# The value stage of a mixture-of-experts kernel: weights split by four keys instead of two, and four places for streamed table tiles instead of five

## The chip, the cores and the metric

The kernel runs on one core of a Trainium2 chip. It is timed as device microseconds of one launch. Three timed runs of the kernel before gave a median of 2621.04 us (2620.36 to 2621.34).

## What is computed

One decoder block on 256 tokens of width 2048: gated linear attention and sparse attention side by side, cross-attention to a memory, and a feed-forward layer of single-neuron experts (PEER). The change touches the last step of that layer. Each token chose 16 experts in each of 8 heads out of 128 x 128; its output is the weighted sum of the experts' rows of the table `peer_v` (16384 x 2048):

```python
def block(args):
    xb, eb, gb = args
    act = jax.nn.gelu(jnp.einsum('td,tkd->tk', xb, u_tab[eb]))
    return jnp.einsum('tk,tkd->td', gb * act, v_tab[eb])
```

The last step of the program adds this to the residual and applies an RMSNorm.

## The kernel before

**The value stage.** Most of the output is made without a gather. The table `peer_v` is read as a whole, as 128 tiles of 128 rows by 2048 columns (1024 KB), one for each first-half key j. For each key there is a matrix of weights, 128 rows of the tile by tokens, in `spread` (128 columns) and `spread_shared` (64 more), and TensorE adds up weights times tile into all eight PSUM banks. To keep float32 precision, tile and weights are each split into a high and a low part of the fast matmul type:

- ScalarE writes the tile's high part in two halves (`value_high`, L1355; `v_hi` has two places), VectorE the low part over it (`value_low`, L2425; `v_lo` lies where `v_raw` lay).
- ScalarE writes the high part of the weights (`weights_high`, L1366, copies of L1374), VectorE the low part (`weights_low`, L2431, L2434), into `e_parts`, two batches of BATCH keys each.
- TensorE runs `high_pass(i)` (L1813, 12 matmuls of L1824), then `low_pass(i - 1)` (L1828, 8 matmuls of L1836). The end of a low pass signals `tile_used`: the tile's place is free.

**Who fetches.** SyncE issues the tiles in the order of the keys (L812 to L825). Tile j waits for the low pass of the tile that had its place before (`tiles_freed`), five keys back. The first five wait each for what lay in their place: dots of the stage before, two steps of the octet copies ("unit_spread"), and, for key 4, "seeded", when the residual has been read into the banks.

**The late rows.** For the last four heads of the second 128 tokens, rows are gathered singly: GpSimd issues 64 indirect DMAs for rows of `peer_u` and 64 for rows of `peer_v` (`late_rows`, L884), 128 partitions of 8 KB each, and VectorE works on one of them for nearly every key (`late_step`: a dot product, L2446, or a multiply-add into `hN`, L2453; both a little over 2 us). Rows have three places at first; a fourth opens at row 37 and a fifth at row 71, which lie in `spread_shared` where the weights of the first 32 and 64 keys were. So these two wait for "e_split", which counts batches of weights that are split (`ROWS_GROW`).

**Order on each engine.** It is written out by hand. VectorE at key j: weights of the next batch, if j is the last of its batch; the low part of tile j; the late row. ScalarE at key j: the high part of tile j; then the weights of the next batch, if j is the last of its batch, which waits for the low pass of the batch that had the place before (`tiles_freed` in `weights_high`). A high half of tile i waits for the high pass and for the low part of tile i - 2, whose place in `v_hi` it takes.

```python
V_PLACES = (RAW + 104 * K, HT + 8 * K, HT, MRG + 8 * K, WRK)
```

These are the tiles' five places in SBUF. `e_parts` begins at MRG.

Of the kernel before, what the change touches and what calls it, by code (L numbers as in the profile page):

```python
# [50 lines left out]
GROUPS = TT * PEER_H  # L51
RING = 6
RING_IN_QUERIES = 4
BATCH = 2
VCOLS = D // 2
BANK = 512
LATE = tuple(range(GROUPS - 4, GROUPS))
# [3 lines left out]
SPLIT = tuple(j for j in range(NKEYS) if j not in NATIVE)  # L61
LATE_FROM = 1
LATE_SPAN = NKEYS - 2
ROWS_GROW = {37: 16, 71: 32}
UNIT = 4
SHARED = P // 2
HALF = P // UNIT
# [132 lines left out]
def hybrid_block(nc, a):  # L200
# [4 lines left out]
    def sem(name):  # L205
        if name not in sems:
            sems[name] = ctx.enter_context(nc.semaphore(name))
        return sems[name]

    base = (nc.sbuf_base + 63) // 64 * 64  # L210
    K = 1024

    def sb(name, shape, at, dt=F32):

        return nc.alloc_sbuf_tensor_at("b_" + name, [P] + list(shape), dt, offset=base + int(at))[:]


    RAW, HI, LO, ACTV, ATTN, HT, SCR, MRG, WRK, SML = (0, 32 * K, 48 * K, 64 * K, 96 * K, 128 * K, 144 * K, 160 * K,
                                                       176 * K, 192 * K)
# [86 lines left out]
        + [(SCR, n) for n in range(4)])]  # L306
    e_whole = sb("e_whole", [2, BATCH, 3 * P], MRG)
    e_parts = sb("e_parts", [2, BATCH, 3 * P], MRG, F32R)
    E_HI, E_LO, E_SHARED = slice(0, P), slice(P, 2 * P), slice(2 * P, 3 * P)
    E_SHARED_HI, E_SHARED_LO = slice(2 * P, 2 * P + SHARED), slice(2 * P + SHARED, 3 * P)  # L310
    V_PLACES = (RAW + 104 * K, HT + 8 * K, HT, MRG + 8 * K, WRK)
    v_raw = [sb(f"v_raw{n}", [D], at) for n, at in enumerate(V_PLACES)]
    v_lo = [sb(f"v_lo{n}", [D], at, F32R) for n, at in enumerate(V_PLACES)]
    v_hi = sb("v_hi", [2, D], SCR, F32R)
# [69 lines left out]
    def load_chunk(sp, apart, p, c, w, col):  # L384
        rows = w.rearrange("(q k p) n -> q p k n", q=UQ, p=P)
        for q in range(UQ):
            apart(w_split, unit(p, c, q) - 2 * UQ + 1)
            sp.dma_start(raw[:, UQ * c + q], rows[q][:, :, bass.ds(col, CH)]).then_inc(w_landed[UQ * c + q], 16)

    def load_pair(sp, apart, p, sources):  # L390
        for c, (w, col) in enumerate(sources):
            load_chunk(sp, apart, p, c, w, col)
# [7 lines left out]
    def load_wide(sp, apart, p, w, col):  # L400
        rows = w.rearrange("(u k p) n -> u p k n", u=2 * UQ, p=P)
        for u in range(2 * UQ):
            apart(w_split, unit(p, 0, u) - 2 * UQ + 1)
            sp.dma_start(as_wide(raw[:, u]), rows[u][:, :, bass.ds(col, WIDE)]).then_inc(w_landed[u], 16)
# [268 lines left out]
    def slot_free(s):  # L673

        return max(dotted_at(n) for n in range(EARLY * PTOP) if row_slot[n] == s)
# [12 lines left out]
    def places(count, first, grow):  # L688

        place, back = [], []  # L690
        size = first
        for n in range(count):
            size += n in grow
            place.append(n if n < first else size - 1 if n in grow else place[n - size])
            back.append(size)
        return place, back

    tile_place, tile_back = places(NKEYS, len(v_raw), {})
    row_place, row_back = places(LATE_ROWS, 3, ROWS_GROW)

    def landed(sems, place, n):
        return sems[place[n]], 16 * place[:n + 1].count(place[n])
# [8 lines left out]
    def tiles_freed(eng, *tiles):  # L711

        eng.wait_ge(sem("tile_used"), 1 + max(use_order.index(j) for j in tiles))
# [9 lines left out]
    def weights_of(b):  # L723

        split = [j for j in range(b * BATCH, (b + 1) * BATCH) if j not in NATIVE]
        keys = slice(split[0], split[-1] + 1)
        e = e_parts[:, b % 2, split[0] % BATCH:split[-1] % BATCH + 1]
        def by_unit(x):
            return x.rearrange("p i (u t) -> p i u t", t=UNIT)
# [30 lines left out]
    def square(name):  # L760
        return a[name][0]
# [4 lines left out]
    @block.sync  # L766
    def _(sp):
        apart = Apart(sp, w_split)
        for half in range(2):
            d = slice(half * D // 2, (half + 1) * D // 2)  # L770
            sp.dma_start(xN[:, :, d], a["x"][0, :, d].rearrange("(t p) d -> p t d", p=P)).then_inc(sem(f"x_landed{half}"), 16)

        def load_small(dst, name, w, done):
            sp.dma_start(small_w[:, :, dst:dst + w],
                         w_in[:, COL[name]:COL[name] + w].rearrange("(k p) n -> p k n", p=P)).then_inc(done, 16)

        load_small(0, "i_k", IDX_D, sem("keys_in"))
        load_small(P, "d_k", DH, sem("keys_in"))
        load_chunk(sp, apart, IQ, 0, w_in, COL["i_q"])
        load_small(2 * P, "d_v", DH, sem("small_landed"))  # L780
        load_small(3 * P, "i_w", IDX_H, sem("small_landed"))
        load_small(3 * P + IDX_H, "g_low", RANK, sem("small_landed"))
        load_chunk(sp, apart, IQ, 1, w_in, COL["i_q"] + CH)
        load_pair(sp, apart, IQ + 1, [(w_in, COL["i_q"] + (2 + c) * CH) for c in range(2)])

        def stream(first, lo, hi, w, col=0):
            with sp.Fori(lo, hi) as i:
                load_pair(sp, apart, first + i, [(w, i * 2 * CH + col + c * CH) for c in range(2)])

        def gated(first, gate, w):  # L790
            with sp.Fori(0, 4) as i:
                load_wide(sp, apart, i * 2 + first, w_in, i * WIDE + COL[gate])
                load_wide(sp, apart, i * 2 + first + 1, w, i * WIDE)

        stream(DQ, 0, 4, w_in, COL["d_q"])
        gated(GB, "gate_b", square("w_proj_dsa"))
        with sp.Fori(0, GLA_H) as h:
            load_pair(sp, apart, h * 3 + GL, [(w_in, h * DK + COL[n]) for n in ("g_q", "g_k")])
            load_wide(sp, apart, h * 3 + GL + 1, w_in, h * DV + COL["g_v"])
            load_pair(sp, apart, h * 3 + GL + 2, [(w_in, h * DV + COL["g_r"] + c * CH) for c in range(2)])  # L800
        gated(GA, "gate_a", square("w_proj_gla"))
        for first, name in ((XK, "w_xk"), (WO, "w_out")):
            stream(first, 0, 4, square(name))
        with sp.Fori(0, 4) as i:
            load_wide(sp, apart, XV + i, square("w_xv"), i * WIDE)
        for first, name in ((XQ, "w_xq"), (XO, "w_xo"), (PQ, "peer_wq")):
            stream(first, 0, 4, square(name))

        v_rows = a["peer_v"][0]

        for j in range(NKEYS):
            if j == 0:  # L812
                sp.wait_ge(sem("dotted"), slot_free(5))
            if j == 1:
                sp.wait_ge(sem("dotted"), EARLY * PTOP)
            if j == 2:
                sp.wait_ge(sem("unit_spread"), HALF + 4)
            if j == 3:
                sp.wait_ge(sem("unit_spread"), HALF + 8)
            if j == 4:  # L820
                sp.wait_ge(sem("seeded"), 2)
            if j >= tile_back[j]:
                tiles_freed(sp, j - tile_back[j])
            where, count = landed(v_landed, tile_place, j)
            sp.dma_start(v_raw[tile_place[j]], v_rows[j * P:(j + 1) * P]).then_inc(where, 16)  # L825
        sp.wait_ge(sem("late_used"), LATE_ROWS)
        sp.dma_start(gfin, a["norm_final_g"].partition_broadcast(P)).then_inc(sem("final_gain_landed"), 16)
        for t in range(TT):
            for n in range(4):
                sp.wait_ge(sem("out_ready"), 4 * t + n + 1)  # L830
                sp.dma_start(a["out"][0, t * P:(t + 1) * P, n * 512:(n + 1) * 512], hN[:, t, n * 512:(n + 1) * 512]
                             ).then_inc(sem("out_stored"), 16)
        sp.wait_ge(sem("out_stored"), 16 * TT * 4)
# [3 lines left out]
    def _(pool):  # L837
# [46 lines left out]
        def late_rows(lo, hi):  # L884

            pool.wait_ge(sem("dotted"), slot_free(4) if hi == 1 else EARLY * PTOP)
            for m in range(lo, hi):
                g, kind, k = LATE[m // (2 * PTOP)], m // PTOP % 2, m % PTOP
                if m in ROWS_GROW:
                    pool.wait_ge(sem("e_split"), ROWS_GROW[m])  # L890
                elif m >= 3:
# [19 lines left out]
    def _(act):  # L911
# [454 lines left out]
        def weights_high(b):  # L1366

            if b >= 2:
                tiles_freed(act, *range((b - 2) * BATCH, (b - 1) * BATCH))
            for j in range(b * BATCH, (b + 1) * BATCH):  # L1370
                if j in NATIVE:
# [1198 lines left out]
```

## Time and profile before

| | |
|---|---|
| median of three runs | 2621.04 us |
| the profiled execution | 2621.42 us, its span 2619.7 us |
| TensorE matmul busy | 2308.6 us (88%) |
| VectorE busy | 2026.9 us (77%) |
| ScalarE busy | 1304.5 us (50%) |
| GpSimd busy | 655.9 us (25%) |
| DMA moved | 729.10 MB, mean 278 GB/s |
| value stage | about 1966 to 2601 us of the span |

The profile is one execution. "Idle before" names the engine or DMA that ended an instruction's wait. A DMA's "us to landing" counts from its issue on the queue to its last byte's signal, so it holds the time in which it queues behind other transfers. In the timeline a row of SPq is the issue alone.

### The profile page before, as it was taken

The numbers are of one execution on the slowest core, as the hardware profiler recorded it, in microseconds if no ns is written. First come the engines' busy times: TensorE is split into PE (matmuls) and PEld (weight loads), VectorE is DVE, ScalarE is ACT, GpSimd is POOL, SyncE is SP. The second block draws the span as 40 slices with busy tenths as digits, with TensorE's granted clock in tenths as the row PEclk, the third lists the DMA queues.
The fourth block names the chain that finished last, engine by engine and source line by source line (L and its number), as shares of the span: only waits on it lengthen the run. The fifth ranks groups of instructions, "written<-read, shape, count | busy, mean of one in ns | idle before, by whom it ended". The sixth has DMA issues, their size and how long they took to land.

```text
span 2619.7 us, 35803 instructions
## 1 busy us (share of the span) xinstructions
PE 2308.6 (88%) x13097; PEld 2021.1 (77%) x13097; DVE 2026.9 (77%) x2622; ACT 1304.5 (50%) x2085; POOL 655.9 (25%) x339
## 2 busy tenths in 40 slices
PE   8999999999999999999999775536329999999997
PEld 7998889999988888889989765435227777777775
DVE  7786556667655755664467999999999999999999
ACT  4555544444444543454355324887645444444444
POOL 1000000000000000010001577886853343345331
PEclk9999999999999999999999987666659999999999
DMA  7444665554566555564457999999989999999997
GB/s 232 147 141 142 193 193 169 161 161 149 172 213 186 182 189 187 175 208 154 144 178 268 356 394 414 421 422 391 408 313 395 421 421 421 421 419 421 421 421 310
DMA packets 273975, 729.10 MB, mean 278 GB/s; under 512 B 21192, under 2 KB 164768, under 8 KB 215856
## 3 DMA queue, kind: packets, MB, share of 16 engines
q1 hardware_dynamic: 226432, 385.65, 42.8%
q0 software_dynamic: 46912, 340.81, 31.9%
q8 instruction: 85, 1.39, 0.2%
q10 hardware_dynamic: 496, 0.84, 0.1%
q14 instruction: 50, 0.41, 0.0%
HBM read 725.14 MB, written 2.10 MB: 278 GB/s over the span
## 4 chain that ended last, share of the span: by engine, by line
PE 57%; DMA 20%; DVE 16%; ACT 3%; POOL 3%; issue 2%; SPq 0%; DVEq 0%; ACTq 0%; POOLq 0%
PE bank L429 20%; PE bank L451 15%; PE bank L478 10%; DMA b_v_raw<-in_peer_v 7%; DVE b_u_ring L2368 7%; DMA b_late_row<-in_peer_v,b_idx_all 5%; DMA b_late_row<-in_peer_u,b_idx_all 4%; DMA b_u_ring<-in_peer_u,b_idx_all 3%; PE bank L1824 3%; POOL b_u_ring L880 2%; PE bank L1836 2%; DVE b_late_row L2446 1%; PE bank L1613 1%; DVE b_hN L2453 1%; DVE b_v_lo L2429 1%
## 5 line engine op out<-in xcount | busy, mean ns | idle before, releaser
L415 DVE TENSOR_TENSOR b_w_both<-b_raw,b_w_both 128x1024 fp32r<-128x1024 f32 x464 | 564.0, 1234 | 422.2 <-ACT b_w_both L410 421.1
L410 ACT ACTIVATE b_w_both<-b_raw 128x1024 fp32r<-128x1024 f32 x464 | 483.4, 1057 | 538.7 <-PE bank L429 215.1
L880 POOL DMA_INDIRECT b_u_ring<-in_peer_u,b_idx_all x192 | 381.9, 1989 | 159.5 <-DVE b_dots L2368 75.3
L1824 PE MATMUL bank<-b_v_hi,b_e_parts 128*128 128x512 f32 x1536 | 385.0, 397 | 33.0 <-DVE b_e_parts L2434 20.8
L1364 ACT ACTIVATE b_v_hi<-b_v_raw 128x1024 fp32r<-128x1024 f32 x254 | 255.2, 1052 | 307.8 <-DVE b_v_lo L2429 158.7
L2368 DVE CUSTOM_DVE_ANT_0 b_u_ring<-b_u_ring,b_xnN 128x2048 f32<-128x2048 f32 x172 | 390.7, 2278 | 12.9 <-DMA b_u_ring<-in_peer_u,b_idx_all 12.7
L1824 PEld LDWEIGHTS bank<-b_v_hi,b_e_parts 128*128 128x128 f32 x1536 | 283.4, 189 | 122.4 <-issue 33.0
L429 PE MATMUL bank<-b_w_both,b_act_both 128*128 128x512 f32 x1536 | 353.7, 390 | 0.0
L429 PEld LDWEIGHTS bank<-b_w_both,b_act_both 128*128 128x128 f32 x1536 | 287.3, 188 | 59.3
L451 PE MATMUL bank<-b_act_both,b_w_both 128*128 128x256 f32 x2688 | 329.1, 284 | 0.0
L451 PEld LDWEIGHTS bank<-b_act_both,b_w_both 128*128 128x128 f32 x2688 | 324.4, 192 | 1.6 <-issue 1.3
L2429 DVE TENSOR_TENSOR b_v_lo<-b_v_raw,b_v_hi 128x2048 fp32r<-128x2048 f32 x128 | 291.9, 2281 | 0.0
L1836 PE MATMUL bank<-b_v_lo,b_e_parts 128*128 128x512 f32 x1024 | 253.4, 390 | 0.0
L1836 PEld LDWEIGHTS bank<-b_v_lo,b_e_parts 128*128 128x128 f32 x1024 | 192.4, 188 | 40.7
L451 PE MATMUL bank<-b_att_both,b_w_both 128*128 128x256 f32 x1536 | 188.3, 284 | 0.0
L451 PEld LDWEIGHTS bank<-b_att_both,b_w_both 128*128 128x128 f32 x1536 | 185.5, 192 | 0.2
L478 PE MATMUL bank<-b_act_both,b_w_both 128*128 128x512 f32 (+1 forms) x1024 | 181.6, 338 | 0.0
L429 PE MATMUL bank<-b_w_both,b_att_both 128*128 128x512 f32 x768 | 177.1, 392 | 0.0
L478 PEld LDWEIGHTS bank<-b_act_both,b_w_both 128*128 128x128 f32 x1024 | 158.2, 190 | 21.7
L894 POOL DMA_INDIRECT b_late_row<-in_peer_v,b_idx_all x64 | 125.3, 1957 | 191.9 <-DVE b_hN L2453 135.8
L894 POOL DMA_INDIRECT b_late_row<-in_peer_u,b_idx_all x64 | 120.5, 1883 | 206.5 <-DVE b_dots L2446 140.3
L429 PEld LDWEIGHTS bank<-b_w_both,b_att_both 128*128 128x128 f32 x768 | 145.2, 189 | 30.7 <-issue 0.3
(326 smaller groups left out, 2504.3 us busy)
## 6 DMA issues: line engine op xcount, KB each, us to landing
b_v_raw<-in_peer_v SPq DMA_DIRECT2D x128, 1024.0 KB, 11.1
b_raw<-in_w_in SPq DMA_DIRECT2D x208, 512.0 KB, 4.6
b_raw<-in_w_proj_dsa SPq DMA_DIRECT2D x32, 512.0 KB, 4.9
b_raw<-in_w_proj_gla SPq DMA_DIRECT2D x32, 512.0 KB, 4.0
b_raw<-in_w_xk SPq DMA_DIRECT2D x32, 512.0 KB, 3.4
b_raw<-in_w_out SPq DMA_DIRECT2D x32, 512.0 KB, 3.4
b_raw<-in_w_xv SPq DMA_DIRECT2D x32, 512.0 KB, 4.4
b_raw<-in_w_xq SPq DMA_DIRECT2D x32, 512.0 KB, 4.2
```

The costliest lines, as they stand in the source:

```text
L410: act.activation(w_hi[:, q], raw[:, UQ * c + q], ACT.Copy).then_inc(w_high, 1)
L415: dve.tensor_tensor(w_lo[:, q], raw[:, UQ * c + q], w_hi[:, q].bitcast(F32), ALU.subtract).then_inc(w_split, 1)
L429: mm = pe.matmul(bank[pair[t]], x[:, kt, t * P:(t + 1) * P], as_wide(w_both[:, half, u % UQ])[:, k], start=(kt == 0 and half == 0 and x is ...
L451: mm = pe.matmul(proj[c][:, n], w[:, q, k, n * P:(n + 1) * P], x[:, kt, :], start=(q == 0 and n == 0 and k == 0 and w is w_hi and x is hi) ...
L478: mm = pe.matmul(twin[c][n] if wide else twin[c][n][:, 0], *pair, start=wide and first, stop=not wide and last, skip_group_check=True)
L880: pool.indirect_dma_start(u_ring[:, s], None, u_rows, bass.IndirectOffsetOnAxis(ap=idx_all[:, at:at + 1], axis=0)).then_inc(u_landed[s], 16)
L894: pool.indirect_dma_start(late_row[row_place[m]], None, (u_rows, a["peer_v"][0])[kind], bass.IndirectOffsetOnAxis(ap=idx_all[:, g * PTOP + ...
L1364: act.activation(v_hi[:, v_place(i), c], v_raw[tile_place[j]][:, c], ACT.Copy).then_inc(sem("v_high"), 1)
L1824: mm = pe.matmul(value_bank(e is E_SHARED, v, m), e_parts[:, j // BATCH % 2, j % BATCH, e], v_hi[:, v_place(i), c:c + BANK], start=False, ...
L1836: mm = pe.matmul(value_bank(e is E_SHARED, v, m), e_parts[:, j // BATCH % 2, j % BATCH, e], v_lo[tile_place[j]][:, c:c + BANK], start=Fals ...
L2368: dve.tensor_tensor_reduce(u, u, xnN[:, g // PEER_H], 1.0, 0.0, ALU.mult, ALU.add, dots[:, g * PTOP + k:g * PTOP + k + 1]).then_inc(sem("d ...
L2429: dve.tensor_tensor(v_lo[tile], v_raw[tile], v_hi[:, v_place(i)].bitcast(F32), ALU.subtract).then_inc(sem("v_split"), 1)
```

## The change

Batches of weights hold four keys instead of two. `e_parts` becomes 12 KB instead of 6 and reaches into the place at MRG + 8 K, so this place for tiles goes away and four are left. The wait that stood ahead of the fourth tile ("unit_spread", 8 octets) goes with it, and "seeded" stands ahead of key 3 instead of key 4. The counts at which rows 37 and 71 get their places are converted to batches of four. No arithmetic changes, and no transfer is added or removed.

```diff
-BATCH = 2
+BATCH = 4
...
-ROWS_GROW = {37: 16, 71: 32}
+ROWS_GROW = {37: 32 // BATCH, 71: 64 // BATCH}
...
-    V_PLACES = (RAW + 104 * K, HT + 8 * K, HT, MRG + 8 * K, WRK)
+    V_PLACES = (RAW + 104 * K, HT + 8 * K, HT, WRK)
...
             if j == 2:
                 sp.wait_ge(sem("unit_spread"), HALF + 4)
             if j == 3:
-                sp.wait_ge(sem("unit_spread"), HALF + 8)
-            if j == 4:
                 sp.wait_ge(sem("seeded"), 2)
             if j >= tile_back[j]:
                 tiles_freed(sp, j - tile_back[j])
```

SyncE's queue at the start of the value stage, keys 0 to 6, before (`b_v_raw_147` to `_151` are the tiles' five places; the semaphore waited for stands in brackets):

```order
L825 DMA b_v_raw_147<-in_peer_v 128x2048 [waits dotted]
L825 DMA b_v_raw_148<-in_peer_v 128x2048 [waits dotted]
L825 DMA b_v_raw_149<-in_peer_v 128x2048 [waits unit_spread]
L825 DMA b_v_raw_150<-in_peer_v 128x2048 [waits unit_spread]
L825 DMA b_v_raw_151<-in_peer_v 128x2048 [waits seeded]
L825 DMA b_v_raw_147<-in_peer_v 128x2048 [waits tile_used]
L825 DMA b_v_raw_148<-in_peer_v 128x2048 [waits tile_used]
```

And of the change:

```order
L823 DMA b_v_raw_147<-in_peer_v 128x2048 [waits dotted]
L823 DMA b_v_raw_148<-in_peer_v 128x2048 [waits dotted]
L823 DMA b_v_raw_149<-in_peer_v 128x2048 [waits unit_spread]
L823 DMA b_v_raw_150<-in_peer_v 128x2048 [waits seeded]
L823 DMA b_v_raw_147<-in_peer_v 128x2048 [waits tile_used]
L823 DMA b_v_raw_148<-in_peer_v 128x2048 [waits tile_used]
L823 DMA b_v_raw_149<-in_peer_v 128x2048 [waits tile_used]
```

Key 3's tile now stands behind "seeded", and key 4's is the first that waits for a low pass, where key 5's was; each later issue waits for the same low pass as before with the next key's tile.

ScalarE from the first batch of weights on, before (`b_e_parts<-b_spread` and `<-b_spread_shared` are the weights' high parts, `b_v_hi` the tiles'):

```order
L1374 ACTIVATE b_e_parts<-b_spread 128x2x128 [waits spread_copied]
L1374 ACTIVATE b_e_parts<-b_spread_shared 128x2x64
L1364 ACTIVATE b_v_hi<-b_v_raw_148 128x1024 [waits v_landed1]
L1364 ACTIVATE b_v_hi<-b_v_raw_148 128x1024
L1374 ACTIVATE b_e_parts<-b_spread 128x2x128
L1374 ACTIVATE b_e_parts<-b_spread_shared 128x2x64
L1364 ACTIVATE b_v_hi<-b_v_raw_149 128x1024 [waits v_split,v_high_used,v_landed2]
L1364 ACTIVATE b_v_hi<-b_v_raw_149 128x1024
L1364 ACTIVATE b_v_hi<-b_v_raw_150 128x1024 [waits v_split,v_high_used,v_landed3]
L1364 ACTIVATE b_v_hi<-b_v_raw_150 128x1024
L1374 ACTIVATE b_e_parts<-b_spread 128x2x128 [waits tile_used]
L1374 ACTIVATE b_e_parts<-b_spread_shared 128x2x64
```

And of the change (lines are two lower):

```order
L1372 ACTIVATE b_e_parts<-b_spread 128x4x128 [waits spread_copied]
L1372 ACTIVATE b_e_parts<-b_spread_shared 128x4x64
L1362 ACTIVATE b_v_hi<-b_v_raw_148 128x1024 [waits v_landed1]
L1362 ACTIVATE b_v_hi<-b_v_raw_148 128x1024
L1362 ACTIVATE b_v_hi<-b_v_raw_149 128x1024 [waits v_split,v_high_used,v_landed2]
L1362 ACTIVATE b_v_hi<-b_v_raw_149 128x1024
L1362 ACTIVATE b_v_hi<-b_v_raw_150 128x1024 [waits v_split,v_high_used,v_landed3]
L1362 ACTIVATE b_v_hi<-b_v_raw_150 128x1024
L1372 ACTIVATE b_e_parts<-b_spread 128x4x128
L1372 ACTIVATE b_e_parts<-b_spread_shared 128x4x64
L1362 ACTIVATE b_v_hi<-b_v_raw_147 128x1024 [waits v_split,v_high_used,v_landed0]
L1362 ACTIVATE b_v_hi<-b_v_raw_147 128x1024
```

The second batch's pair has moved behind key 3's high part, pairs are twice as wide, and the pair that waited for "tile_used" ahead of key 4's high part is gone.

## Rows read from the trace of the kernel before

**Rows 1.** The page's GB/s moved, in 40 equal slices of the span.

```profile
GB/s 232 147 141 142 193 193 169 161 161 149 172 213 186 182 189 187 175 208 154 144 178 268 356 394 414 421 422 391 408 313 395 421 421 421 421 419 421 421 421 310
```

**Rows 2.** Stretches: us; busy PE, PEld, DVE, ACT, POOL (instructions); PEclk, DMA share, GB/s.

```profile
1948.00:1956.00 8.00, 8.00 (x50) 8.00 (x50) 7.32 (x29) 3.18 (x6) 0.00 (x0) 0.67 0.19 52
1956.00:1964.00 8.00, 8.00 (x70) 7.93 (x70) 8.00 (x30) 6.81 (x13) 1.47 (x2) 1.00 0.65 244
...
1972.00:1976.00 4.00, 4.00 (x19) 3.33 (x18) 4.00 (x3) 2.01 (x2) 1.80 (x1) 1.00 0.37 109
1976.00:1984.00 8.00, 8.00 (x37) 6.62 (x36) 8.00 (x9) 3.06 (x5) 3.79 (x3) 1.00 0.99 399
1984.00:2100.00 116.00, 110.08 (x474) 87.86 (x473) 109.69 (x83) 54.00 (x73) 43.54 (x23) 1.00 1.01 422
...
2400.00:2500.00 100.00, 96.52 (x404) 73.91 (x403) 95.51 (x73) 45.72 (x62) 36.58 (x20) 1.00 1.01 421
...
2593.00:2599.00 6.00, 5.84 (x25) 4.33 (x24) 6.00 (x4) 3.27 (x4) 0.00 (x0) 1.00 0.33 132
```

**Rows 3.** Timeline of SyncE's queue, 1957 to 1976 us: start, us, what.

```profile
1957.65 0.33 SPq L825 DMA_DIRECT2D b_v_raw<-in_peer_v  x1
...
1966.95 7.62 SPq L825 DMA_DIRECT2D b_v_raw<-in_peer_v  x2
```

**Rows 4.** Chain of waits, 2400 to 2425 us: start, us, what.

```profile
2399.04 13.86 DMA b_v_raw<-in_peer_v
...
2412.92 1.07 ACT b_v_hi L1364
...
2414.12 2.97 PE bank L1824 x12
2417.10 1.83 PE bank L1836 x8
...
2418.94 13.84 DMA b_v_raw<-in_peer_v
```

**Rows 5.** Value tiles landing, in 1930-2060, 1976-2000, 2100-2150, 2400-2500; a DMA issue.

```profile
DMA to landing us min/median/max: 6.8/10.0/11.2
...
DMA to landing us min/median/max: 8.4/8.4/8.4
...
DMA to landing us min/median/max: 10.0/10.1/10.3
...
DMA to landing us min/median/max: 13.8/13.8/13.9
...
b_gfin<-in_norm_final_g SPq DMA_DIRECT2D x1, 1024.0 KB, 4.7
```

**Rows 6.** Timeline, 2000 to 2040 us (as rows 3; idle before in brackets).

```profile
2003.89 2.01 ACT L1364 ACTIVATE b_v_hi<-b_v_raw 128x1024 fp32r<-128x1024 f32 x2 [4.44 <-DVE b_v_lo L2429]
...
2013.99 2.00 PE L1836 MATMUL bank<-b_v_lo,b_e_parts 128*128 128x512 f32 x8
...
2015.82 2.88 PE L1824 MATMUL bank<-b_v_hi,b_e_parts 128*128 128x512 f32 x12
```

**Rows 7.** Timeline at the stage's start, then VectorE from 1989 us.

```profile
1965.77 0.42 ACT L1374 ACTIVATE b_e_parts<-b_spread 128x256 fp32r<-128x256 f32 x1
1966.09 0.29 ACT L1374 ACTIVATE b_e_parts<-b_spread_shared 128x128 fp32r<-128x128 f32 x1
...
1966.29 1.99 ACT L1364 ACTIVATE b_v_hi<-b_v_raw 128x1024 fp32r<-128x1024 f32 x2
...
1989.90 0.42 DVE L2434 TENSOR_TENSOR b_e_parts<-b_spread,b_e_parts 128x256 fp32r<-128x256 f32 x1
...
1990.49 2.28 DVE L2429 TENSOR_TENSOR b_v_lo<-b_v_raw,b_v_hi 128x2048 fp32r<-128x2048 f32 x1
```

**Rows 8.** Who waited for whom, 1966 to 2600 us: total, times, longest.

```profile
PE bank L1824 <- DVE b_e_parts L2434: 20.8, 25, 5.5
```

**Rows 9.** Timeline of GpSimd, 2120 to 2180 us.

```profile
2139.59 2.42 POOL L894 DMA_INDIRECT b_late_row<-in_peer_u,b_idx_all  x1 [0.30 <-issue]
```

## The prediction

> **What bounds the kernel now.** I read the page's row of GB/s first: the DMA engines move more in the last third than anywhere else and stand at 421 GB/s for most of it [rows 1]. The table of stretches says from when: they move 52 GB/s from 1948 to 1956 us, 244 from 1956 to 1964, 109 from 1972 to 1976, then 399, and from 1984 on 421 to 422 with a share of 1.01, up to the last tiles at 2593 [rows 2]. So ahead of about 1976 us the engines have holes, and behind it none. The value stage takes, for each key, one tile of 1024 KB by SyncE's queue and, nearly always, one late row of the same size by GpSimd's: 2.10 MB at 421 GB/s are 4.98 us. The chain of waits shows the same pace from the other side: from the issue of one tile to the issue of the one four keys on are 19.90 us [rows 4], 4.975 us a key. In it a tile is under way for 13.86 us; the other 6.04 are ScalarE's first half (1.07), the high pass (2.97), the low pass of the key before (1.83) and gaps, and that low pass frees the place of the next issue. PE's part, 2.97 + 1.83 = 4.80 us, is shorter than 4.975, and VectorE is busy for 95.51 of 100 us there [rows 2]; both come close, neither is the bound.
>
> **The change part by part.** (a) *One place less at the start.* Before, the tile of key 3 has its place from the octet copies and is issued at 1957.65; key 4 and key 5 follow at 1966.95 and some 7.3 us later [rows 3]. The changed SyncE queue waits for "seeded" with key 3 (1966.95) and for the first low pass with key 4. All later issues stand where they stood, each with the next key's tile, so the stage has one tile less in hand. What was moved at 1957.65 was moved in a hole, and the engines have another hole at 1972 to 1976 after it [rows 2], so nothing queued behind makes up for it. One tile more must then be moved in the stretch without holes: 1.049 MB / 421 GB/s = 2.49 us. The bounds are 0, if the tile is caught up somewhere, and 4.98 us, if it costs a whole key. A gain is excluded, as no transfer is removed. I take 2.5, since what follows runs at 421 GB/s throughout.
>
> (b) *The first batch is twice as wide.* PE's first high pass waits for ScalarE's two copies. They start at 1965.77 and 1966.09, the next instruction at 1966.29 [rows 7]: 0.52 us the pair, 0.42 for 256 columns and 0.29 for 128. By that, 128 columns cost 0.13, and twice the width adds 0.26 + 0.13 = 0.39 us (bounds 0 and 0.52). PE starts that much later, and so do the first low pass and the issue that waits for it; the hole at 1972 grows. I take +0.4 us.
>
> (c) *Fewer and wider splits later.* Of 64 pairs each, 32 go away on ScalarE and 32 on VectorE. On VectorE a pair takes 0.59 us, from 1989.90 to 1990.49 [rows 7]; a merged pair costs between 0.59 and 1.18 in place of 1.18. Taking the middle, VectorE gains 0.3 us every four keys, some 9 us in all. ScalarE no longer waits for the tile of two keys back ahead of the split, but for that of four back, long done. PE waits 20.8 us in the stage for the weights' low parts [rows 8], and some of that goes. None of it reaches the end: the cover is the DMA at 4.975 us a key. I cost it at 0. If that cover were gone, it would be a gain of up to 9 us. In turn a merged split holds VectorE's and ScalarE's queues for up to twice as long once in four keys; queued behind it are the key's value split, its late row and the next key's high half. The low pass that needs the value split runs only after the next key's high pass, so that costs 0 too.
>
> (d) *One tile less in the loop.* This is the term on which the forecast stands. Before, the loop is 13.86 + 6.04 us for four keys; after, it closes over three, so the pace holds if a tile lands within 3 x 4.975 - 6.04 = 8.9 us. In the first half the chain is another: VectorE waits for late rows, ScalarE reads a tile at 2003.89 and its low pass is over at 2015.82, about 12 us [rows 6]; tiles land in 10.1 us and then wait [rows 5]. With four places 4 x 4.975 - 12 = 7.9 us are left. What is the landing time when one tile less is queued? The bounds are 4.7 us (the final gain, of the same size, on idle engines [rows 5]) and 13.86, as now. I take 8.9 and 7.9, no loss: the landing time beyond 4.7 is queueing at engines that are full, and it is the remainder of the loop, not its cause. It was 8.4 in the stage's first 24 us, with the same two queues but a shorter backlog, and 6.8 for the quickest tile [rows 5]. With one tile less, 4.975 us of waiting per tile go away, and about one to two tiles and two rows are still queued. The engines idle only if both queues run empty, and then a landing is short. Cost 0; the high end is a rival below.
>
> The Trainium skill, page "DMA: Bandwidth & Descriptors", section "Queues, rings and completion order", says that each DMA engine goes round-robin between the rings it has work for. By that rule SyncE's tile gets at least every second turn, and an estimate for a tile that finds its own ring empty is 2.5 us more than on idle engines, 7.2 us, under both limits. No row here shows the turns; the rule speaks for (d).
>
> (e) *Late rows 37 and 71.* They wait for the same keys' weights, now 8 batches of four in place of 16 of two, reached up to two keys earlier. GpSimd issued row 37 at 2139.59 after 0.30 us of its own issue, not of a wait [rows 9]: 0.
>
> **Sum.** 2.5 + 0.4 = +2.9 us. The profiled execution took 2621.42 us (span 2619.70), 0.38 above the median of the three timed runs; 2624.3 against it, 2623.9 against the median. A measurement of this kernel can tell about 0.2% (5.2 us) from no change, so this counts as no change.
>
> **The rivals.** *Slower: the tile stream runs out in the first half.* Mechanism: the 12 us hold of rows 6 stays, and a landing takes longer than 7.9 us because late rows keep the engines' turns. At 8.4 us a key takes (8.4 + 12)/4 = 5.10 us, 0.13 more, over 60 keys +8: 2632. At 10.1, as now, 5.5 us a key and +33 us: 2657. For it: the margin is thin (7.9 against 8.4 measured), and four keys' splits at once make the loop uneven. Against it: the engines would have to idle while tiles take as long as on full ones, and part of the 12 us is slack, as PE waits there for weights. It decides where the first half's DMA share drops below 1.0. Chance 0.20, most of it at the low end.
>
> *Faster: the instructions saved count.* If a full DMA share only reflects the pace that VectorE sets, the stage gains the 9 us of (c), less the 2.9: 2615. The Trainium skill, page "VectorE: DVE Perf Modes", section "The TRN2 errata — SBUF-src ops pay a fixed extra latency per instruction", says each such instruction carries a fixed cost, which merging saves; its (N+151)/0.96 ns fits the 0.42 us of 256 columns. An estimate by it is 0.31 us for each four keys. Against it: 422 GB/s is the most that any slice of the page shows [rows 1], and late in the stage ScalarE waits for tiles, not for VectorE, in the chain [rows 4]. Chance 0.04.
>
> *The lost tile is caught up.* PE's and VectorE's free 0.2 us a key can't bring bytes back, but the end can: if the last tile lands as early as now, 2621. It counts as no change, within the forecast's 0.76.
>
> **How the numbers follow.** Forecast 0.76 (within 0.2%), slower 0.20, faster 0.04. The range goes from 2620.5, a lost tile that costs nothing, to 2632, the slower rival at 8.4 us; that leaves out the faster rival and the slower one's upper part.
>
> **What would show it.** Right: the share stays 1.01 from 1984 on; the tiles' landing time falls to about 8 us in the first half and 9 in the second, and is no longer 13.8; three tiles to a loop of 14.9 us; issue of key 3's tile at about 1967; PE's first high pass 0.4 us later, the end 2 to 3 us later; VectorE's busy time down by some 9 us with no gain from it. Wrong: a DMA share under 1.00 in any stretch of the stage, ScalarE waiting more than 3 us for a tile, landing times still over 10 us, or a stage that ends earlier.

## The result, and the profile after

The changed kernel took 2653.86 us (four runs, 2650.71 to 2656.78), the kernel before 2620.70 (four runs, 2619.64 to 2621.34): a ratio of 1.0123 with a 95% interval of 1.0109 to 1.0136. It is slower, well beyond what can be told from no change, and lies outside the range. The profiled execution took 2650.71 us, its span is 2648.9.

First the page's GB/s of the changed kernel, in 40 slices, which answers to [rows 1], and its row for the tiles' issues (the last number is the median time from issue to landing, over the tiles whose landing the profile could match to an issue; it was 11.1 before):

```profile
GB/s 224 150 135 145 192 194 166 156 159 168 149 228 185 183 190 186 189 191 153 141 182 309 340 396 410 421 421 376 404 286 413 398 417 413 406 422 420 411 404 276
...
b_v_raw<-in_peer_v SPq DMA_DIRECT2D x128, 1024.0 KB, 9.7
```

The value stage is the last ten slices. Before, they stood at 421; now at 398 to 422. The stretches of the stage (columns as in [rows 2]):

```profile
1972.00:1976.00 4.00, 3.67 (x16) 1.93 (x15) 3.03 (x5) 3.67 (x6) 2.51 (x1) 1.00 0.79 274
1976.00:1984.00 8.00, 8.00 (x37) 6.62 (x36) 7.54 (x6) 4.37 (x6) 2.74 (x1) 1.00 0.62 248
...
1984.00:2100.00 116.00, 106.48 (x449) 83.85 (x448) 104.76 (x72) 47.36 (x56) 41.17 (x23) 0.99 1.00 410
2100.00:2200.00 100.00, 92.25 (x388) 71.00 (x386) 91.15 (x61) 43.37 (x50) 44.11 (x21) 1.00 1.00 408
...
2300.00:2400.00 100.00, 91.64 (x383) 70.14 (x382) 92.94 (x65) 41.57 (x47) 38.98 (x21) 1.00 1.01 416
2400.00:2500.00 100.00, 92.62 (x392) 71.72 (x391) 92.29 (x56) 44.31 (x50) 39.01 (x20) 1.00 1.01 416
```

Two columns have to be read together here. The DMA share stays at 1.00 to 1.01, as before, and yet only 408 to 416 GB/s are moved. From 2400 to 2500, TensorE is busy for 92.62 us in place of 96.52 and VectorE for 92.29 in place of 95.51. No stretch of the stage is spared: each moves 1 to 3% less than before. In slices of 2 us the loss shows as dips (first row 2452 to 2454, then two others):

```profile
2452.00:2454.00 2.00, 1.50 (x7) 0.95 (x7) 2.00 (x2) 1.35 (x2) 1.75 (x1) 1.00 1.03 430
2454.00:2456.00 2.00, 2.00 (x9) 1.62 (x10) 2.00 (x2) 0.66 (x1) 0.53 (x1) 1.00 0.92 315
...
2460.00:2462.00 2.00, 2.00 (x11) 1.65 (x10) 2.00 (x2) 0.41 (x1) 2.00 (x1) 1.00 0.94 295
```

Of the 250 slices of 2 us from 2000 to 2500, 16 move less than 360 GB/s in the changed kernel and 1 in the kernel before. Among its nine slices from 2446 to 2464 the lowest is

```profile
2452.00:2454.00 2.00, 1.84 (x9) 1.23 (x7) 2.00 (x2) 1.28 (x2) 0.00 (x0) 1.00 0.96 401
```

The chain of waits of the changed kernel in the place of [rows 4] (start, us, what):

```profile
2396.71 9.20 DMA b_v_raw<-in_peer_v
...
2405.93 1.07 ACT b_v_hi L1362
...
2407.14 2.97 PE bank L1822 x12
2410.11 1.83 PE bank L1834 x8
...
2411.95 8.98 DMA b_v_raw<-in_peer_v
...
2426.97 10.41 DMA b_v_raw<-in_peer_v
...
2443.45 9.18 DMA b_v_raw<-in_peer_v
```

The loop has the shape that was predicted: a landing, then the same 6.04 us as before, and it now closes over three keys. From issue to issue are 15.24, 15.02 and 16.48 us; over the whole stretch 46.74 us for nine keys, 5.19 a key. In the first half the chain mostly takes another way (2047 to 2063 is again a loop over three), over four keys, with two pairs of passes between a landing and the issue:

```profile
2090.51 10.04 DMA b_v_raw<-in_peer_v
...
2101.77 3.01 PE bank L1822 x12
2104.78 1.81 PE bank L1834 x8
2106.60 2.72 PE bank L1822 x12
2109.32 1.83 PE bank L1834 x8
...
2111.16 9.28 DMA b_v_raw<-in_peer_v
```

That is 10.04 us and 10.61 of hold, 20.65 us for four keys, 5.16 a key; not the 12 us of hold of [rows 6]. The landing times in the windows of [rows 5], 1976-2000, 2100-2150 and 2400-2500, are

```profile
DMA to landing us min/median/max: 9.1/9.1/9.1
...
DMA to landing us min/median/max: 9.3/10.2/11.1
...
DMA to landing us min/median/max: 9.2/9.6/10.4
```

These rows hold only the tiles whose landing the profile could match to an issue: 1 of 4, 2 of 10 and 5 of 20. The landing of every tile can be read in two other ways, which agree: from the 4-byte signal packets that end each transfer on the queue (16 a tile), and, in the changed kernel, from ScalarE's start on the tile, which follows the landing by 0.02 us when it waits for it. So read, all ten tiles from 2100 to 2150 took 8.0 to 11.1 us with a median of 9.0 (before: 10.2), and all twenty from 2400 to 2500 took 8.3 to 10.4 us with a median of 9.1 (before: 13.8). Over keys 8 to 123 the mean is 9.4 us in each half of the stage, where it had been 10.6 in keys 8 to 67 and 13.3 behind them. From a tile's landing to the issue three keys on are 6.2 us in the mean. Last, who waited for whom, 1966 to 2630 us (total, times, longest):

```profile
ACT b_v_hi L1362 <- DMA b_v_raw<-in_peer_v: 367.5, 125, 6.9
...
PE bank L1822 <- ACT b_v_hi L1362: 47.6, 77, 1.9
DVE b_e_parts L2432 <- ACT b_e_parts L1372: 40.0, 31, 3.1
...
PE bank L1822 <- DVE b_e_parts L2432: 0.3, 1, 0.3
```

ScalarE now waits for nearly every tile (before: 147.4 us, 56 times), and PE behind it (before 11.8 us). The wait of [rows 8] is gone, 20.8 us to 0.3, and nothing was gained by it.

**Where the 29.2 us of span lie.** I count from the start of the stage's first high pass, 1966.44 before and 1974.52 after. So 8.1 us lie ahead of the stage, and 21.1 in it (653.3 us became 674.4). Between the issues of key 8's tile and key 127's are 596.1 us before and 616.9 after: 119 keys at 5.009 and at 5.184 us, +20.8. Both terms vary by some us from one profile of the same kernel to the next, as the second profile of the change shows below. From the first high pass to key 8's issue are 27.8 us instead of 21.4, and from key 127's issue to the end 29.7 instead of 35.8, since a tile is now issued one place later and lands sooner; these two cancel but for 0.3 us.

### The profile page after: what moved, and what is told of

The parts are those of the page before. It is cut to its first block and busy times, and to the rows that moved or that the text cites. A ratio compares the mean times of both kernels' runs of the same rounds, so it can differ in the third digit from the quotient of the medians.

```text
span 2648.9 us, 35675 instructions
## 1 busy us (share of the span) xinstructions
PE 2313.5 (87%) x13097; PEld 2020.5 (76%) x13097; DVE 2022.2 (76%) x2558; ACT 1296.3 (49%) x2021; POOL 656.4 (25%) x339
## 5 line engine op out<-in xcount | busy, mean ns | idle before, releaser
L878 POOL DMA_INDIRECT b_u_ring<-in_peer_u,b_idx_all x192 | 370.2, 1928 | 177.2 <-DVE b_dots L2366 91.4
L892 POOL DMA_INDIRECT b_late_row<-in_peer_u,b_idx_all x64 | 129.0, 2015 | 204.1 <-DVE b_dots L2444 139.9
```

The lines of the kernel that those rows point to most:

```text
L878: pool.indirect_dma_start(u_ring[:, s], None, u_rows, bass.IndirectOffsetOnAxis(ap=idx_all[:, at:at + 1], axis=0)).then_inc(u_landed[s], 16)
L892: pool.indirect_dma_start(late_row[row_place[m]], None, (u_rows, a["peer_v"][0])[kind], bass.IndirectOffsetOnAxis(ap=idx_all[:, g * PTOP + ...
```

## The experiments

**Theory P (places):** the loop over three keys that four places leave can't keep the DMA engines full, as the landing time doesn't shrink to what the loop allows. **Rival B (batch):** a batch of four holds ScalarE, and behind it the tile's high part, at the wrong moment. **Rival S (sharing):** the landing is stretched by the late rows, and the tiles would be served better otherwise. In what follows "the stage" is the time from the first high pass to the end of the span, 653.3 us before and 674.4 after, and the pace is taken from key 8 to key 127.

**Four places, batches of two.** From the kernel before:

```diff
-    V_PLACES = (RAW + 104 * K, HT + 8 * K, HT, MRG + 8 * K, WRK)
+    V_PLACES = (RAW + 104 * K, HT + 8 * K, HT, WRK)
...
             if j == 3:
-                sp.wait_ge(sem("unit_spread"), HALF + 8)
-            if j == 4:
                 sp.wait_ge(sem("seeded"), 2)
```

> The kernel before with four places for tiles and batches of two keys: one half of the change alone. Theory P (the places): in the profile of the change a key takes 5.18 us of the tile stream's issues from key 8 to key 127, against 5.01 before, since the loop over three keys is 9.5 + 6.04 = 15.5 us; batches play no part. So this kernel shows 5.15 to 5.2 us a key, landings of 9 to 10 us, and costs 18 to 24 us in the stage; with the later start of the stage, 2640 to 2655. Theory B (the batches: at every fourth key ScalarE's and VectorE's splits stand between the landing and the next work): this kernel keeps 5.0 us a key and comes out at 2621 to 2626.

Measured: 2646.01 us (2641.41 to 2648.21) against 2621.34, ratio 1.0094 (1.0077 to 1.0111). The stage takes 674.4 us, the same as in the changed kernel, and its stretches from 2100, 2200 and 2300 show the same loss at a share of 1.00 or more:

```profile
2100.00:2200.00 100.00, 89.01 (x368) 68.62 (x366) 88.62 (x68) 41.11 (x55) 38.41 (x20) 0.98 1.00 406
2200.00:2300.00 100.00, 91.55 (x384) 72.41 (x385) 91.29 (x64) 45.27 (x61) 34.11 (x19) 0.98 1.00 398
2300.00:2400.00 100.00, 91.25 (x382) 69.91 (x381) 92.34 (x75) 43.00 (x58) 42.30 (x22) 1.00 1.01 420
```

The pace is 5.19 us a key, as expected, and over keys 8 to 123 a tile lands in 9.4 us in the mean. The missing place alone does it, and B is not needed.

**Five places, and only the start as in the change.** From the kernel before; key 4 waits for the first low pass and key 5 for the second:

```diff
             if j == 3:
-                sp.wait_ge(sem("unit_spread"), HALF + 8)
-            if j == 4:
                 sp.wait_ge(sem("seeded"), 2)
+            if j == 4:
+                tiles_freed(sp, 0)
+            if j == 5:
+                tiles_freed(sp, 1)
```

> The kernel before with its five places, but key 3's tile is issued only when the banks are seeded, key 4's after the first low pass and key 5's after the second, as in the change: only the start has one tile less in hand, the steady loop keeps five places. The prediction's term for the start says +2.5 us, about 2623.5, and 5.0 us a key as before. If the loss at the start is what the whole stage never catches up, it is more, up to +8.

Measured: 2623.55 us (10 runs) against 2621.34, ratio 1.0008 (0.9996 to 1.0021), the stage 656.2 us, 2.9 more than before. The engines are full from then on, and tiles land in 13.8 us:

```profile
2400.00:2500.00 100.00, 96.60 (x403) 73.92 (x403) 95.75 (x72) 45.84 (x62) 36.60 (x20) 1.00 1.01 421
```

and the tiles' landing times from 2400 to 2500:

```profile
DMA to landing us min/median/max: 13.8/13.8/13.8
```

The 2.9 us are close to the 2.5 that were predicted, but stages of one kernel differ as much between profiles, and the interval of the ratio holds 1. So one tile less at the start costs a few us at most; the loss is in the loop.

**The change, with the weights' high part ahead of the tile's on ScalarE**, to test B from the other side:

```diff
         for j in range(NKEYS):
-            if j in SPLIT and j != SPLIT[0]:
-                value_high(SPLIT.index(j))
             if j % BATCH == BATCH - 1 and j + 1 < NKEYS:
                 weights_high((j + 1) // BATCH)
+            if j in SPLIT and j != SPLIT[0]:
+                value_high(SPLIT.index(j))
```

> The change, but ScalarE makes the high parts of the next four keys' weights ahead of the tile's high part, while it waits for the tile anyway, so VectorE's 40 us of waits for them go away. Theory B: most of the loss in the stage comes back, 5.0 us a key, some 2633. Theory P: the tile stream's loop doesn't hold these instructions, 5.15 to 5.2 us a key stay, within 4 us of the change.

Measured: 2641.16 us, 1.0081 (1.0064 to 1.0098); the stage 666.5 us, 7.9 less than in the changed kernel's profile and 4.9 less than in its second one below. Landings are 9.2 us in the mean, and the pace is 5.11 us a key, between what the two theories gave (5.0 and 5.15 to 5.2). Other kernels with the changed kernel's loop came as near (1.0065, 1.0090 and 1.0097 below), so no more than a few us can be its own, and most of the loss stays.

**The change without the late rows**, for the pace that the engines could keep:

```diff
                 elif m >= 3:
-                    pool.wait_ge(sem("late_used"), m - row_back[m] + 1)
+                    continue
...
-            dve.wait_ge(*landed(late_landed, row_place, m))
+            if m < 3:
+                dve.wait_ge(*landed(late_landed, row_place, m))
+            else:
+                dve.wait_ge(sem("late_used"), m - 2)
             if kind == 0:
-                dve.tensor_tensor_reduce(row, row, xn_late, 1.0, 0.0, ALU.mult, ALU.add, dots[:, k:k + 1]
+                dve.tensor_tensor_reduce(row, row if m < 3 else xn_late, xn_late, 1.0, 0.0, ALU.mult, ALU.add, dots[:, k:k + 1]
```

> The change without the late rows' transfers from the fourth row on (their vector work stays, on other data): what it leaves out is 125 gathers of 1 MB, so its output has wrong values in the late heads. The tile stream has the engines to itself. A landing should be near the 4.7 us of an idle transfer, so the loop over three keys would allow 3.6 us a key, and the pace is that of the engines that compute: 4.55 to 4.75 us a key from key 8 to 127, which says how fast a stall can be caught up, 0.2 to 0.4 us a key.

(`ROWS_GROW` is empty here too, since no row waits for a place.) Measured: 2579.66 us (two runs), 0.9833 (0.9806 to 0.9861), and from 2400 on

```profile
2400.00:2500.00 100.00, 98.26 (x428) 79.71 (x427) 99.97 (x71) 47.46 (x56) 0.00 (x0) 1.00 0.63 222
```

and the tiles' landing times from 2400 to 2500:

```profile
DMA to landing us min/median/max: 4.6/4.8/6.1
```

VectorE is the bound there, at 99.97 of 100 us, with 4.54 to 4.75 us a key. Two things follow. A tile that has the engines nearly to itself lands in 4.8 us with four places too; without the rows' traffic the rest of 9.4 is gone. And compute has only 0.2 to 0.4 us a key in hand under 4.975; an estimate from that is that it takes about three to five keys to catch up after a landing that is 1 us late.

**The change, each tile in two transfers of 512 KB**, with the first high half waiting for its half alone; cut to its core:

```diff
-            sp.dma_start(v_raw[tile_place[j]], v_rows[j * P:(j + 1) * P]).then_inc(where, 16)
+            right = right_landed(j)[0]
+            for v, done in ((0, where), (1, right)):
+                c = slice(v * VCOLS, (v + 1) * VCOLS)
+                sp.dma_start(v_raw[tile_place[j]][:, c], v_rows[j * P:(j + 1) * P, c]).then_inc(done, 16)
...
+                if v:
+                    act.wait_ge(*right_landed(j))
```

> The change, but each tile comes in two transfers of 1024 columns, and ScalarE starts on the first half when that has landed. Between the landing of the whole tile and the issue of the next one there are then the second half's copy (1.05), the second half of the high pass (1.45) and the low pass (1.83), 4.4 us instead of 6.04. Theory P: the loop over three keys falls by 1.6 us, under the DMA's pace, so a key takes 4.98 to 5.05 us and the stage gives back 16 to 24 us. Theory B, or engines that are simply full: no change beyond 3 us, or slower for the extra transfers.

Measured: 2668.60 us, 1.0178 (1.0161 to 1.0195): worse, where I had expected a gain. Its stretches from 2300 and 2400 are among those that move 380 to 400 GB/s:

```profile
2300.00:2400.00 100.00, 83.52 (x339) 64.60 (x338) 80.75 (x61) 40.90 (x46) 34.50 (x19) 0.97 0.97 380
2400.00:2500.00 100.00, 91.01 (x387) 71.25 (x386) 91.92 (x54) 44.24 (x48) 40.93 (x19) 1.00 1.01 400
```

A whole tile lands 10.3 us after its first half's issue, in the mean, and the time from there to the issue three keys on is 6.0 us, not 4.4; so the loop got longer and not shorter. The same edit on the kernel before:

> The kernel before (five places, batches of two) with each tile in two transfers of 1024 columns, so in descriptors of 4 KB, half as long as the late rows'. The change with the same edit took 2668.6 us, 15 more, at 375 to 400 GB/s. Theory S (the engines take turns between the two queues by descriptor, so the tile stream's share falls with the length of its descriptors, and the stream that everything waits for gets less): five places have slack for longer landings, GB/s stay near 415 to 421 where they hold, and the total is 2620 to 2640. Theory W (descriptors of 4 KB are moved at a worse rate whoever waits): GB/s fall to about 400 here too, 5.2 us a key, 2650 or more.

Measured: 2634.75 us, 1.0051 (1.0037 to 1.0064). Its engines have a share of 1.02, and move less:

```profile
2200.00:2300.00 100.00, 93.10 (x394) 74.20 (x394) 92.97 (x65) 47.99 (x62) 49.60 (x20) 0.98 1.02 413
2300.00:2400.00 100.00, 88.91 (x373) 70.02 (x372) 90.42 (x72) 43.97 (x58) 35.66 (x20) 0.98 1.02 415
```

The halves make pieces of 4 KB where a tile has 8 KB. With five places they move 412 to 415 GB/s instead of 421, a little under the 415 to 421 of theory S and well over the 400 of theory W; the total falls in the range of theory S. It doesn't decide between the two. Whether reading the first half sooner gains anything can't be told from this pair, as the rate fell at the same time.

**The change, every odd tile issued on ScalarE's queue** two keys ahead of its use, so that the tiles have two queues against the late rows' one (rival S):

```diff
-            if j >= tile_back[j]:
+            if j >= tile_back[j] and not j % 2:
                 tiles_freed(sp, j - tile_back[j])
+            if j % 2 and j >= tile_back[j]:
+                continue
...
+            n = j + 2
+            if n % 2 and tile_back[n % NKEYS] <= n < NKEYS:
+                tiles_freed(act, n - tile_back[n])
+                act.dma_start(v_raw[tile_place[n]], a["peer_v"][0][n * P:(n + 1) * P]).then_inc(landed(v_landed, tile_place, n)[0], 16)
```

> The change, but from key 5 on the tiles of odd keys are issued on ScalarE's queue, right behind the high part of two keys before; even ones stay on SyncE's. The places, the batches and the bytes are those of the change. Theory S: with two rings against the late rows' one the tiles get up to two turns in three, landings fall from 9.5 towards 8 us, a key takes 5.0 to 5.08 us, some 2635 to 2643. If the turns play no part and the loop of four places alone sets the pace, nothing changes: 5.15 to 5.2 us a key.

Measured: 2672.03 us, 1.0191 (1.0167 to 1.0214). Its chain:

```profile
2400.27 1.53 ACT b_v_hi L1364 x2
2401.80 8.63 DMA b_v_raw<-in_peer_v
...
2410.45 0.43 ACT b_v_hi L1364
2410.88 9.85 DMA b_v_raw<-in_peer_v
...
2420.75 1.06 ACT b_v_hi L1364
2421.81 10.34 DMA b_v_raw<-in_peer_v
```

From key 8 to key 127 a key takes 5.34 us, more than either side of the expectation. The tiles' landings didn't shorten (9.3 us in the mean of keys 8 to 123, 9.4 in the change), and from a landing to the issue three keys on are now 6.8 us instead of 6.2: half of the issues stand behind ScalarE's own work. In this form a second queue does harm. It doesn't decide how much the late rows take.

**The change, with the low pass ahead of the high pass** (and the weights first on ScalarE, as above, since the low pass now comes sooner). This gives back one key of the loop with four places: the place of key j - 1 is free without the high pass of key j.

```diff
                 i = SPLIT.index(j)
-                high_pass(i)
                 if i > 0:
                     low_pass(i - 1)
+                high_pass(i)
```

> The change with four places and batches of four, weights ahead of the tile on ScalarE as in e3_weights_first, and TensorE runs the low pass of the key before ahead of the high pass of this key, so the place comes free before the next tile's landing and not after its high pass. The place loop then has four keys for 13.7 us of landing and 6.2 us of work instead of three keys for 8.9 and 6.04. Theory P: the DMA's pace comes back, 421 GB/s and 4.98 to 5.02 us a key, 2615 to 2628, with no place more. If something else than the return of places holds the change back, it stays at 5.08 us a key or above, 2640.

Measured: 2623.41 us (10 runs), 1.0004 (0.9991 to 1.0016), no difference from the kernel before. The stretch and the chain of 2400:

```profile
2400.00:2500.00 100.00, 96.01 (x404) 74.07 (x403) 95.39 (x62) 44.34 (x50) 29.50 (x20) 1.00 1.01 421
```

```profile
2403.43 13.34 DMA b_v_raw<-in_peer_v
...
2417.76 1.05 ACT b_v_hi L1362
...
2418.84 2.30 DVE b_v_lo L2427
...
2421.19 2.12 PE bank L1834 x8
...
2423.33 13.34 DMA b_v_raw<-in_peer_v
```

Four places, batches of four, late rows and queues are those of the change; only the loop is a key longer, 19.90 us for four keys. The landing is 13.34 us, and the engines stand at 421 GB/s again. The order on ScalarE can't be what did it, as that alone (the third experiment) left the pace at 5.11. This is the run that the verdict rests on. The same edit on the kernel before, without the part on ScalarE:

> The kernel before with its five places and batches of two, and TensorE's low pass ahead of the high pass, as in e8_low_first. The loop of places gets slacker still, but the DMA already runs at 421 GB/s, so theory P and the DMA's bound together say no change: 5.0 us a key, 2618 to 2626. If it were clearly faster, the place loop would have held back the kernel before as well.

Measured: 2618.04 us (10 runs) against 2622.09, 0.9985 (0.9976 to 0.9995), with landings of 17.1 to 17.7 us from 2400 to 2500 (the profile matched 4 of 20; all of them: 16.1 to 17.8). It is the fastest kernel of this study that does all the work, by 0.15%, within what counts as no change here.

**The change and the four places once more**, side by side, as the first two had been timed apart. The first is the changed kernel unedited; the second is the first experiment's kernel.

> The change itself once more, beside four places alone on the same chip, to see what the batches of four add. In the two profiles so far both take 617 us from key 8's issue to key 127's, so the batches add nothing there; the medians, from different calls, stand 8 us apart (2653.9 and 2646.0). If the batches cost nothing, this one comes out within 4 us of four places alone; if the bursts of four late rows cost, it is 5 to 10 us slower.

> Four places and batches of two, as in e1_places4, beside the change: 2640 to 2650, with 5.15 to 5.2 us a key. See e10_change_again for what the difference decides.

Measured: the change 2643.47 us (6 runs, 2639.23 to 2652.42), 1.0090 (1.0071 to 1.0108); four places alone 2644.86 us (2641.87 to 2651.94), 1.0097 (1.0079 to 1.0114). Batches of four cost and bring nothing that can be measured. In the first of these profiles the first high pass starts at 1967.48, and the stage takes 671.4 us, at 5.16 us a key; it is the same kernel that had 1974.52, 674.4 and 5.18 above. So the change costs 21 to 33 us by the medians, and the smaller figure too lies outside the range of the prediction.

**The change, with three places for late rows throughout**, so that fewer rows are queued beside the tiles:

```diff
-ROWS_GROW = {37: 32 // BATCH, 71: 64 // BATCH}
+ROWS_GROW = {}
```

> The change with three places for late rows throughout, instead of four from row 37 and five from row 71: fewer gathers queue on the engines beside the tiles. If the tile's landing of 9.5 us, 0.6 above what the loop has room for, comes from gathers running ahead into their spare places, landings fall to 9 or below in the second half and a key there takes 5.0 to 5.05 us: 2630 to 2638. If the spare places play no part (the change's own trace has 5.17 us a key with three and 5.2 with five), it stays at 5.15 to 5.2 us a key, 2640 to 2655; if both streams together now queue too little to keep the engines fed, it is slower than the change, above 2655.

Measured: 2639.94 us (6 runs, 2634.30 to 2655.96), 1.0065 (1.0039 to 1.0092), whose interval overlaps that of the change's second timing; it lies at the lower edge of what was expected if the spare places play no part. In its profile the stage takes 677.3 us, at 5.20 us a key:

```profile
2300.00:2400.00 100.00, 90.88 (x376) 71.60 (x375) 91.63 (x66) 42.41 (x49) 42.36 (x21) 0.97 0.99 400
2400.00:2500.00 100.00, 92.33 (x394) 72.61 (x393) 91.36 (x55) 43.12 (x48) 36.16 (x19) 1.00 0.99 405
```

and the tiles' landing times from 2400 to 2500:

```profile
DMA to landing us min/median/max: 8.2/9.5/10.3
```

These are 10 of the 20 tiles. The mean of keys 8 to 123 is 9.2 us against 9.4: tiles land hardly sooner, so the fourth and fifth place for rows are not what keeps them there. That the rows' traffic as a whole matters was shown by the kernel without it (4.8 us).

## Why the prediction was wrong

**The step that failed is (d)**, "the landing time beyond 4.7 is queueing at engines that are full, and it is the remainder of the loop, not its cause". The budget itself was right: 8.9 us for a loop over three keys. Above it the statement held late in the stage: with five places, or with four and the low pass first, the landing fills up whatever the loop leaves, 13.8, 13.3 and 17.3 us, always at 421 GB/s. But the landing does not fall freely to any smaller remainder. At a budget of 8.9 it stayed at 9.4 us in the mean of the stage, and the time of work grew from 6.04 to 6.2: (9.4 + 6.2) / 3 = 5.2 us a key, against 5.184 measured. That sum comes out for any loop whose two parts are measured; what shows that the loop's length is the cause is the pair of four places alone (5.19 us a key) and of the low pass first (421 GB/s again, 5.03 us a key). 119 keys at 0.175 us more are the 20.8 us.

I had 8.9 and 4.7 before me and took the budget as its own proof, because "the engines idle only if both queues run empty". The dips to 295 and 315 GB/s say that they move less already with 1.8 tiles in flight (9.4 / 5.18; it was 13.8 / 4.975 = 2.8 before). And the 8.4 us that I set beside the budget, "in the stage's first 24 us", were one matched tile of five; all five took 8.4 to 10.5 us, with a median of 9.6. Read so, the rows of before already spoke against 8.9 and 7.9.

**(a) and (b), the start: no sign against them.** The kernel with only the start changed was 2.9 us longer in the stage, against 2.5 for (a); its median is 2.2 us above, with an interval that holds no difference. For (b), ScalarE's two copies take 0.84 us to the next instruction instead of 0.52, +0.3 against 0.39.

**(c), the splits: right at 0.** A merged pair on VectorE takes 0.95 us in place of 1.18; VectorE's busy time fell by 4.7 us, not 9, and nothing came of it. The rows of the merged pair, with the idle time before it:

```profile
2403.83 0.69 DVE L2432 TENSOR_TENSOR b_e_parts<-b_spread,b_e_parts 128x512 fp32r<-128x512 f32 x1 [1.33 <-ACT b_e_parts L1372]
2404.44 0.42 DVE L2432 TENSOR_TENSOR b_e_parts<-b_spread_shared,b_e_parts 128x256 fp32r<-128x256 f32 x1
```

The 0.69 us of 512 columns agree with the formula of the Trainium skill, page "VectorE: DVE Perf Modes", section "The TRN2 errata — SBUF-src ops pay a fixed extra latency per instruction", (512 + 151) / 0.96 = 691 ns. I missed that VectorE now waits for the high parts of the weights, 40.0 us in all, because ScalarE writes the tile's high part first and waits for the tile to land. The kernel with the weights first took this wait away and gained a few us at most.

**(e): not tested by itself.** Without the two row places the profile's stage is no shorter, so these rows cost nothing that showed.

**The slower rival** had the mechanism (tiles take longer to land than the loop allows). That its +33 us for a landing of 10.1 equals the 33.2 us between the first medians is luck: it was for the first half alone, at 5.5 us a key and 12 us of hold, while 8.1 of the measured us lie ahead of the stage, and the second timing of the same kernel gave 21.4. It also had the place and one sign to watch wrong. The loss is not that of the first half: the pace is 5.17, 5.17, 5.21 and 5.18 us a key in the four parts of the stage, and the second half lost as well. And the share never fell clearly under 1.00 in any stretch of the table, by which it was to be told; the sign that did come was ScalarE waiting up to 6.9 us for a tile. I gave it 0.20, and let the range end at its cheap end, 8.4 us, which stood on the one matched tile.

**The faster rival** fell: the instructions saved gave nothing. The rule that I had set beside (d), from the Trainium skill, page "DMA: Bandwidth & Descriptors", section "Queues, rings and completion order", led to an estimate of 7.2 us for a tile that finds its ring empty. Tiles took 8.3 to 10.4 us late in the stage; from 2400 to 2500 the quickest in the kernel with the weights first took 6.8. No run shows the turns of the queues. With 1.8 tiles in flight a tile mostly has another ahead of it in its ring, so that the estimate was for a case that hardly occurs.

**What stays open.** Why the landing settles at 9.4 us in the mean and not at 8.9: two ways to relieve the queues were tried (fewer places for rows, a second queue for tiles), and neither lowered it by more than 0.2 us. One reading is that single landings are uneven by about 1 us, that in a loop without slack a late one is not made up, as compute can catch up only 0.2 to 0.4 us a key, and that the engines then lack work for a moment; this fits the runs and was not shown by itself. Nor is it settled why the first four timings of the change were 10 us above the six later ones, or why the first high pass starts anywhere from 1962.6 to 1974.5 in the fourteen profiles. As the changed kernel itself had 1974.5 and 1967.5, most of the 8.1 us ahead of the stage belong to the execution; whether the change has a part in them isn't shown.

## What to carry to other kernels

When a buffer is taken from a stream that runs at full DMA rate, work out what landing time the loop that is left allows, and test it against the landing time that the stage shows under load, not against the one that would just fit; here 8.9 us allowed was too tight and 13 was ample. See how many transfers a row of landing times covers before a bound is taken from it. Read GB/s, not the DMA share, to see whether the engines are full, and ask whether compute has the speed to make up for one late landing. Here, freeing a place one step earlier in TensorE's order was worth as much as a place of 8 KB a partition.

## What the runs showed of the hardware

- A DMA share of 1.00 to 1.01 went with 408 to 417 GB/s in the two profiles of the change, with 398 to 420 with four places alone, and with 421 before; with tiles in halves and five places, a share of 1.02 with 412 to 415. So in these traces the share doesn't tell how many bytes move.
- Pieces of 4 KB instead of 8 for half of the traffic went with 1.4 to 2.1% less rate with five places (412 to 415 against 421 GB/s), and with more loss where the stream was on the path (380 to 400 against 408 to 416).
- Tiles spread over two queues didn't land sooner: 7.1 to 11.3 us against 8.3 to 10.4 from 2400 to 2500, and the kernel took 1.0191 times as long as the one before.
- With the late rows' gathers beside them, tiles of 1024 KB landed in 9.4 us in the mean with four places and in 13.8 us late in the stage with five; without the gathers, in 5.0 us.
